# Moving the rounded activations of the down products to other SBUF addresses in a two-layer encoder kernel

## The chip, the cores and the metric

The kernel runs on one NeuronCore of a Trainium2 chip. The metric is the device time of one execution in microseconds (us), median of the runs shown. Addresses in this text are bytes inside one SBUF partition; every tile spans all 128 partitions.

## The reference

256 tokens of width 1024 pass through two layers and a final norm, all in float32. What the change touches are the two feed-forward blocks, and in them the last product.

```python
def swiglu(h, w_gate, w_up, w_down):
    return (jax.nn.silu(h @ w_gate) * (h @ w_up)) @ w_down

def moe_swiglu(h, w_router, b_router, w_gate, w_up, w_down):
    logits = (h @ w_router).astype(jnp.float32) + b_router.astype(jnp.float32)
    top_v, top_i = lax.top_k(logits, TOP_K)            # TOP_K = 2
    top_w = jax.nn.softmax(top_v, axis=-1)
    combine = jnp.sum(jax.nn.one_hot(top_i, N_EXPERTS, dtype=jnp.float32) * top_w[..., None], axis=-2).astype(h.dtype)
    out = jnp.zeros_like(h)
    for e in range(N_EXPERTS):                          # 8 experts
        out = out + combine[..., e:e + 1] * swiglu(h, w_gate[e], w_up[e], w_down[e])
    return out
```

Layer 0 is retention, then the dense `swiglu` with 2816 hidden columns. Layer 1 is attention, then `moe_swiglu` with 3584 hidden columns in each of the 8 experts. Each sub-block is preceded by an RMS norm with a shift and a scale computed from `c`, and its result is gated and added to `x`.

## The kernel before, in words

**Products.** A float32 product is made of three float32r matmuls. The weight tile that came from HBM (`stage`) is rounded by ScalarE to `hi`, and VectorE writes the rest, `lo = stage - hi`. Activations are split the same way, into `..._hi` and `..._lo`. `three` (lines 2006 to 2008) then issues activation-hi x weight-hi, activation-hi x weight-lo and activation-lo x weight-hi into one PSUM bank. In each of them the activation block, 128x128, is the stationary operand, which TensorE loads ahead (the PEld rows), and the 512 columns of `hi` or `lo` are the moving operand. So each matmul of 512 columns is paired with one load of 128x128.

**Units and rings.** Weights arrive in units of 1 MB (128 partitions x 2048 float32). SyncE issues each as two DMAs into one of the 6 slots of `stage` once TensorE has counted that slot free on the semaphore `w_used` (lines 471 to 475); `lo` lies in the same slots, and `hi` has homes of its own (`hi`, and in the expert stage also `hi_m`, `hi_h`, `hi_r`). A unit is 12 matmuls in the expert stage and 24 in the dense layer.

**Dense layer.** The 2816 hidden columns go in 11 chunks of 256, each with two units of gate and up weights and one of down weights. Per chunk (`f_chunk`): gate and up products with `hT_hi`, `hT_lo`, the down products of the chunk before with `faT_hi`, `faT_lo` (24 matmuls, `f_down`), and four transposes of the new hidden values (`f_turn`). ScalarE turns the transposes into `faT_hi` (`f_high_act`, line 954), VectorE into `faT_lo` (`f_low_act`, line 1534). The last chunk uses homes of its own, `faT2_hi` and `faT2_lo`.

**Experts.** Each expert has 7 chunks of 512 hidden columns, 56 in all, and its at most 128 tokens are gathered into `hg_hi`, `hg_lo`. Per chunk: four units of gate and up products (48 matmuls, `e_gate_up`), two units of down products of the chunk before (24 matmuls, `e_down_step`) with `eaT_hi`, `eaT_lo` as stationary operand, and four transposes (`e_turn`, line 2430). ScalarE writes `eaT_hi` (`e_high_act`, line 1135), VectorE writes `eaT_lo` (`e_low_act`, line 1820). The very last chunk uses `eaT2_hi`, `eaT2_lo`.

**Addresses.** Every tile is put at a fixed address by `at(name, shape, offset)`, the offset counted in float32 words from `base`. `R` is the offset of the big work area, and `KW` is 256 words (1024 bytes). A line asserts the place of that area in the pattern of 128 bytes:

```python
base = (nc.sbuf_base + 31) // 32 * 32 + 64
...
assert (base + 4 * R) % 128 == 64
```

With the numbers of this build `base` is 16576, which also leaves 64 when divided by 128. So `stage`, `lo`, `hi`, `hi_m`, `hi_h`, `hi_r`, `hT`, `hg`, `faT` and `eaT` all start 64 bytes into a block of 128 bytes, and so does each of their 512-byte and 2048-byte pieces. Stationary and moving operand of each product therefore start at the same place of that pattern.

Of the kernel before, what the change touches and what calls it, by code (L numbers as in the profile page):

```python
# [10 lines left out]
SEQ = 256  # L11
# [15 lines left out]
F32R = mybir.dt.float32r  # L27
# [29 lines left out]
SLOTS = 128  # L57
# [56 lines left out]
def encoder(nc, x, l0_ada_w, l0_ada_b, l0_norm2_g, l0_ret_w_in, l0_ret_decay_logit,  # L114
# [5 lines left out]
    with ctx:  # L120
# [3 lines left out]
        def at(name, shape, offset, dt=F32):  # L124
            return nc.alloc_sbuf_tensor_at(name, [P] + shape, dt, offset=base + 4 * offset)
# [48 lines left out]
        R = top[0]  # L174
        KW = 256
# [22 lines left out]

        fsil = at("fsil", [TT, FCH], R + 16 * KW)
        fact = at("fact", [TT, FCH], R + 18 * KW)  # L200
        faT_hi = at("faT_hi", [2, SEQ], R + 20 * KW, F32R)
        faT_lo = at("faT_lo", [2, SEQ], R + 22 * KW, F32R)
        faT2_hi = at("faT2_hi", [2, SEQ], R + 24 * KW, F32R)
        faT2_lo = at("faT2_lo", [2, SEQ], R + 26 * KW, F32R)
        hi_q = at("hi_q", [UW], R + 36 * KW, F32R)
# [38 lines left out]
        hi_r = at("hi_r", [UW], R + 24 * KW, F32R)  # L244
        esil = at("esil", [ECH], R + 34 * KW)
        eact = at("eact", [ECH], R + 36 * KW)
        eaT_hi = at("eaT_hi", [4, SLOTS], R + 38 * KW, F32R)
        eaT_lo = at("eaT_lo", [4, SLOTS], R + 40 * KW, F32R)
        dn_hi = at("dn_hi", [D], R + 42 * KW, F32R)
        dn_lo = at("dn_lo", [D], R + 46 * KW, F32R)  # L250
        dnw = [at("dnw0", [CB], R + 34 * KW), at("dnw1", [CB], R + 36 * KW)]
# [2333 lines left out]
```

## Time and profile before

| | us |
|---|---|
| median of 3 runs (1546.7 to 1549.3) | 1547.74 |
| the profiled execution, its device time | 1551.42 |
| span of its instructions | 1549.5 |
| TensorE busy, share of the span | 1496.9, 97% |
| VectorE busy | 1334.4, 86% |
| ScalarE busy | 983.8, 63% |
| moved by DMA | 508.71 MB |

The profile is of one execution, 3.7 us longer than the median; 1.9 us of its time lie outside the span. Stages, read from the timeline: retention to about 258 us, dense layer to about 458 us, attention and router to about 567 us, experts to about 1536 us, then the combination and the final norm. A busy time of TensorE is the union of records that overlap: each matmul of 512 columns has a record of 0.39 us, while they start 0.23 us apart. So the start times tell the pace, and the busy share does not.

### The profile page before, as it was taken

The page shows a single profiled execution, that of the slowest core. Times are in us where ns is not written, and L with a number is a line of the kernel's source. Part 1 is how long each engine was busy: PE and PEld are TensorE (multiplying, and loading weights), DVE is VectorE, ACT ScalarE, POOL GpSimd, SP SyncE. Part 2 cuts the span into 40 slices and gives each one's busy share as a digit, 9 for nine tenths or more (in the row PEclk, how much of TensorE's full clock was granted, in tenths as well). Part 3 has the DMA queues.
Part 4 walks back from the last instruction along what each step waited for, and adds up shares of the span by engine and source line. Part 5 has one row for each costly group of instructions (what it writes and reads, how often), then busy time and mean ns, then how long its engine had stood idle before and what let it go on. Part 6 is the DMA issues. An engine that isn't in the chain of part 4 may idle for free.

```text
span 1549.5 us, 20453 instructions
## 1 busy us (share of the span) xinstructions
PE 1496.9 (97%) x6796; PEld 1220.7 (79%) x6796; DVE 1334.4 (86%) x1072; ACT 983.8 (63%) x814; POOL 212.6 (14%) x188
## 2 busy tenths in 40 slices
PE   7999999999999999999999999999999999999997
PEld 6777677788877787778888888888888887888785
DVE  6899778878889689998988888988988988889898
ACT  4554444443447566677776777777777777777674
POOL 0499700000030011002001002001001000000320
PEclk9999999999999989999999999999999999999999
DMA  9989826898885279999999999999999999999993
GB/s 340 390 303 351 288 87 226 301 307 305 282 275 166 96 283 359 391 346 380 388 368 368 384 370 362 391 370 370 390 367 368 386 367 353 385 381 363 390 392 143
DMA packets 238897, 508.71 MB, mean 328 GB/s; under 512 B 15494, under 2 KB 38150, under 8 KB 238728
## 3 DMA queue, kind: packets, MB, share of 16 engines
q1 hardware_dynamic: 233824, 491.52, 87.2%
q0 software_dynamic: 4448, 14.55, 2.7%
q10 hardware_dynamic: 584, 2.11, 0.3%
q8 instruction: 24, 0.39, 0.1%
q14 instruction: 17, 0.14, 0.0%
HBM read 502.12 MB, written 7.87 MB: 329 GB/s over the span
## 4 chain that ended last, share of the span: by engine, by line
PE 72%; DVE 10%; POOL 7%; DMA 3%; issue 3%; ACT 3%; SPq 1%; DVEq 0%; ACTq 0%; POOLq 0%
PE bank L2006 22%; PE bank L2008 22%; PE bank L2007 22%; DVE lo L1756 3%; PE bank L2430 1%; POOL proj L638 1%; POOL proj L637 1%; DVE lo L1233 1%; POOL ropet L634 1%; POOL ropet L633 1%; POOL ropet L635 1%; POOL proj L636 1%; DMA stage<-in_l_moe_w_up 1%; DMA stage<-in_l_moe_w_gate 1%; PE bank L2112 1%
## 5 line engine op out<-in xcount | busy, mean ns | idle before, releaser
L1756 DVE TENSOR_TENSOR lo<-stage,hi 128x2048 fp32r<-128x2048 f32 x168 | 388.2, 2318 | 44.2 <-ACT hi L1091 43.9
L1091 ACT CAST hi<-stage 128x2048 fp32r<-128x2048 f32 x168 | 321.4, 1914 | 108.3 <-DMA stage<-in_l_moe_w_up 91.8
L2007 PE MATMUL bank<-lo,hg_hi 128*128 128x512 f32 x892 | 347.4, 389 | 0.0
L756 ACT CAST hi<-stage 128x2048 fp32r<-128x2048 f32 x68 | 130.0, 1914 | 108.1 <-PE bank L2008 87.6
L2007 PEld LDWEIGHTS bank<-lo,hg_hi 128*128 128x128 f32 x892 | 167.7, 188 | 33.4
L1233 DVE TENSOR_TENSOR lo<-stage,hi 128x2048 fp32r<-128x2048 f32 x68 | 157.4, 2317 | 24.6 <-ACT hi L756 18.7
L2006 PE MATMUL bank<-hi,hg_hi 128*128 128x512 f32 x448 | 174.5, 389 | 1.4 <-DVE lo L1756 1.4
L2007 PE MATMUL bank<-lo,eaT_hi 128*128 128x512 f32 x448 | 174.4, 389 | 0.0
L2008 PE MATMUL bank<-hi,hg_lo 128*128 128x512 f32 x448 | 174.3, 389 | 0.0
L1756 DVE TENSOR_TENSOR lo<-stage,hi_h 128x2048 fp32r<-128x2048 f32 x56 | 128.3, 2292 | 52.4 <-ACT hi_h L1091 52.2
L2006 PE MATMUL bank<-hi,hT_hi 128*128 128x512 f32 x400 | 162.9, 407 | 2.7 <-DVE hT_lo L1288 2.4
L2007 PE MATMUL bank<-lo,hT_hi 128*128 128x512 f32 x416 | 164.0, 394 | 0.0
L2008 PE MATMUL bank<-hi,hT_lo 128*128 128x512 f32 x400 | 157.6, 394 | 0.0
L1091 ACT CAST hi_r<-stage 128x2048 fp32r<-128x2048 f32 x56 | 107.2, 1913 | 50.4 <-DMA stage<-in_l_moe_w_gate 46.7
L1756 DVE TENSOR_TENSOR lo<-stage,hi_m 128x2048 fp32r<-128x2048 f32 x56 | 128.2, 2290 | 6.3 <-ACT hi_m L1091 5.2
L1756 DVE TENSOR_TENSOR lo<-stage,hi_r 128x2048 fp32r<-128x2048 f32 x56 | 127.9, 2285 | 5.6 <-ACT hi_r L1091 5.3
L1091 ACT CAST hi_m<-stage 128x2048 fp32r<-128x2048 f32 x56 | 107.2, 1915 | 35.1 <-DMA stage<-in_l_moe_w_down 35.0
L1091 ACT CAST hi_h<-stage 128x2048 fp32r<-128x2048 f32 x56 | 107.2, 1913 | 33.6 <-DMA stage<-in_l_moe_w_gate 32.1
L1245 DVE SCALAR_TENSOR_TENSOR ada_acc<-ada_w,cact,ada_acc 128x512 f32<-128x512 f32 x147 | 118.7, 808 | 4.5
L719 POOL DMA_INDIRECT y_rows<-yout,sidx x7 | 10.4, 1484 | 755.3 <-ACT yout L1147 755.3
L2006 PEld LDWEIGHTS bank<-hi,hg_hi 128*128 128x128 f32 x448 | 84.1, 188 | 19.6 <-DVE lo L1756 2.2
L2007 PEld LDWEIGHTS bank<-lo,eaT_hi 128*128 128x128 f32 x448 | 84.2, 188 | 17.6 <-issue 0.5
(367 smaller groups left out, 2793.6 us busy)
## 6 DMA issues: line engine op xcount, KB each, us to landing
stage<-in_l_moe_w_gate SPq DMA_DIRECT2D x224, 512.0 KB, 5.1
stage<-in_l_moe_w_up SPq DMA_DIRECT2D x224, 512.0 KB, 5.7
stage<-in_l_moe_w_down SPq DMA_DIRECT2D x224, 512.0 KB, 5.4
ada_w<-in_l_ada_w SPq DMA_DIRECT2D x40, 1024.0 KB, 5.6
stage<-in_l_ret_w_in SPq DMA_DIRECT2D x48, 512.0 KB, 8.0
stage<-in_l_ffn_w_gate SPq DMA_DIRECT2D x22, 512.0 KB, 7.5
stage<-in_l_ffn_w_up SPq DMA_DIRECT2D x22, 512.0 KB, 8.6
stage<-in_l_ffn_w_down SPq DMA_DIRECT2D x22, 512.0 KB, 8.2
```

What stands on the lines that cost most here:

```text
L633: nc.gpsimd.tensor_tensor(ta, x1, co, ALU.mult)
L634: nc.gpsimd.tensor_tensor(tb, x2, si, ALU.mult)
L635: nc.gpsimd.tensor_tensor(tc, x1, si, ALU.mult)
L636: link(nc.gpsimd.tensor_tensor(x2, x2, co, ALU.mult))
L756: nc.scalar.copy(hi_of(b), stage[:, b % RING, :]).then_inc(hi_done, 1)
L1091: nc.scalar.copy(hi_e(b), stage[:, b % RING, :]).then_inc(hi_done, 1)
L1233: nc.vector.tensor_tensor(lo[:, b % RING, :], stage[:, b % RING, :], hi_of(b).bitcast(F32), ALU.subtract).then_inc(lo_done, 1)
L1245: ins = nc.vector.scalar_tensor_tensor(out=acc, in0=ada_w[:, half, j, :], scalar=cact[:, k:k + 1], in1=acc if k else ada_b[:, :], op0=ALU. ...
L1756: nc.vector.tensor_tensor(lo[:, b % RING, :], stage[:, b % RING, :], hi_e(b).bitcast(F32), ALU.subtract).then_inc(lo_done, 1)
L2006: mm(dst_ap, a_hi, w_hi, start=first, stop=False)
L2007: mm(dst_ap, a_hi, w_lo, start=False, stop=False)
L2008: return mm(dst_ap, a_lo, w_hi, start=False, stop=last)
```

## The change

Four tiles get other addresses; nothing else differs. The instructions of each of the five engines stand in the same order, with the same shapes and the same waits.

```diff
-        faT_hi = at("faT_hi", [2, SEQ], R + 20 * KW, F32R)
-        faT_lo = at("faT_lo", [2, SEQ], R + 22 * KW, F32R)
+        faT_hi = at("faT_hi", [2, SEQ], R + 48 * KW + 16, F32R)
+        faT_lo = at("faT_lo", [2, SEQ], R + 50 * KW + 16, F32R)
...
-        eaT_hi = at("eaT_hi", [4, SLOTS], R + 38 * KW, F32R)
-        eaT_lo = at("eaT_lo", [4, SLOTS], R + 40 * KW, F32R)
+        eaT_hi = at("eaT_hi", [4, SLOTS], R + 58 * KW + 8, F32R)
+        eaT_lo = at("eaT_lo", [4, SLOTS], R + 60 * KW + 8, F32R)
```

| tile | address before | after | place in the 128-byte pattern, before | after |
|---|---|---|---|---|
| `faT_hi` | 184256 | 212992 | 64 | 0 |
| `faT_lo` | 186304 | 215040 | 64 | 0 |
| `eaT_hi` | 202688 | 223200 | 64 | 96 |
| `eaT_lo` | 204736 | 225248 | 64 | 96 |

The moving operands of the same products stay at 64. `faT2` and `eaT2` stay where they were. The tiles whose room is used now (`hi_f` for the dense layer; the router's `wr_hl`, `wr` and `brt`, and a piece of the attention's scratch for the experts) are no longer read when the moved tiles are first written.

## Rows read from the trace of the kernel before

**Rows 1.** The page: busy time, granted clock in 40 slices, chain that ended last.

```profile
PE 1496.9 (97%) x6796; PEld 1220.7 (79%) x6796; DVE 1334.4 (86%) x1072; ACT 983.8 (63%) x814; POOL 212.6 (14%) x188
...
PEclk9999999999999989999999999999999999999999
...
PE 72%; DVE 10%; POOL 7%; DMA 3%; issue 3%; ACT 3%; SPq 1%; DVEq 0%; ACTq 0%; POOLq 0%
```

**Rows 2.** Windows: us, busy of PE, PEld, DVE, ACT, POOL, clock, DMA share, GB/s.

```profile
330.00:440.00 110.00, 110.00 (x487) 89.04 (x486) 88.09 (x81) 44.27 (x37) 5.49 (x7) 1.00 0.89 297
600.00:650.00 50.00, 48.64 (x214) 38.55 (x212) 48.22 (x34) 35.11 (x25) 0.00 (x0) 1.00 1.04 392
1000.00:1100.00 100.00, 99.83 (x459) 82.64 (x458) 87.53 (x51) 74.52 (x51) 4.77 (x6) 1.00 1.02 374
```

**Rows 3.** Waits from 700 to 1500 us: total us, times, longest.

```profile
PE bank L2006 <- DVE lo L1756: 0.9, 1, 0.9
...
SPq L475 <- PE bank L2008: 457.1, 280, 4.2
```

**Rows 4.** Timeline of PE, experts: start us, us, instruction; one chunk's 24 down products.

```profile
1008.00 0.39 PE L2006 MATMUL bank<-hi,eaT_hi 128*128 128x512 f32 x1
1008.23 0.39 PE L2007 MATMUL bank<-lo,eaT_hi 128*128 128x512 f32 x1
1008.46 0.39 PE L2008 MATMUL bank<-hi,eaT_lo 128*128 128x512 f32 x1
...
1013.22 0.39 PE L2008 MATMUL bank<-hi_m,eaT_lo 128*128 128x512 f32 x1
1013.45 0.60 PE L2430 MATMUL bank<-cst,eact 128*128 128x128 f32 x4
```

**Rows 5.** Timeline of PE just behind: the first gate unit after the transposes.

```profile
1013.80 0.48 PE L2006 MATMUL bank<-hi_h,hg_hi 128*128 128x512 f32 x1
1014.12 0.40 PE L2007 MATMUL bank<-lo,hg_hi 128*128 128x512 f32 x1
1014.35 0.40 PE L2008 MATMUL bank<-hi_h,hg_lo 128*128 128x512 f32 x1
1014.59 0.40 PE L2006 MATMUL bank<-hi_h,hg_hi 128*128 128x512 f32 x1
1014.82 0.39 PE L2007 MATMUL bank<-lo,hg_hi 128*128 128x512 f32 x1
1015.04 0.39 PE L2008 MATMUL bank<-hi_h,hg_lo 128*128 128x512 f32 x1
...
1016.43 0.39 PE L2008 MATMUL bank<-hi_h,hg_lo 128*128 128x512 f32 x1
```

**Rows 6.** Timeline of PE, dense layer: first and last of one chunk's 24 down products.

```profile
339.26 0.39 PE L2006 MATMUL bank<-hi,faT_hi 128*128 128x512 f32 x1
...
344.48 0.39 PE L2008 MATMUL bank<-hi,faT_lo 128*128 128x512 f32 x1
```

**Rows 7.** Timeline of PE: float32 records, of 512 columns (dense layer) and of 256.

```profile
327.47 0.59 PE L1984 MATMUL bank<-ada_acc,cst 128*128 128x512 f32 x1
...
344.71 1.02 PE L1984 MATMUL bank<-ada_acc,cst 128*128 128x512 f32 x2
...
494.37 1.89 PE L2278 MATMUL bank<-akT,aqT 128*128 128x256 f32 x8
```

**Rows 8.** Instructions on one tile: count, duration ns min/median/max, first and last start.

```profile
L2007 PE MATMUL bank<-lo,eaT_hi x448: 387/389/397, 592.4 to 1535.6; 128*128 128x512 f32 x150
L2278 PE MATMUL bank<-akT,aqT x32: 377/379/796, 494.4 to 518.3; 128*128 128x256 f32 x32
L1135 ACT CAST eaT_hi<-bank x56: 569/579/594, 581.4 to 1528.1; 128x512 fp32r<-128x512 f32 x56
L1820 DVE TENSOR_TENSOR eaT_lo<-bank,eaT_hi x56: 673/684/693, 587.2 to 1528.8; 128x512 fp32r<-128x512 f32 x56
L1534 DVE TENSOR_TENSOR faT_lo<-bank,faT_hi x11: 683/692/692, 279.5 to 450.1; 128x512 fp32r<-128x512 f32 x11
```

**Rows 9.** Timeline of ACT and DVE: the splits before those down products, and a weight split.

```profile
1000.49 0.58 ACT L1135 CAST eaT_hi<-bank 128x512 fp32r<-128x512 f32 x1
1002.83 0.68 DVE L1820 TENSOR_TENSOR eaT_lo<-bank,eaT_hi 128x512 fp32r<-128x512 f32 x1
1008.44 2.29 DVE L1756 TENSOR_TENSOR lo<-stage,hi_h 128x2048 fp32r<-128x2048 f32 x1 [0.40 <-ACT hi_h L1091]
...
329.30 0.69 DVE L1534 TENSOR_TENSOR faT_lo<-bank,faT_hi 128x512 fp32r<-128x512 f32 x1 [1.76 <-ACT faT_hi L954]
```

## The prediction

> **What bounds the kernel now.** I read the page first: TensorE is busy 97% of the span and holds 72% of the chain that ended last, at nearly the full clock throughout [rows 1]. Busy shares overlap here, so the windows come next: in the dense layer and in the experts' stage TensorE has no idle time, 110.00 of 110 us and 99.83 of 100 us, at a granted clock of 1.00 (2.4 GHz), while VectorE has 12 to 20% left [rows 2]. The waits say who follows whom: from 700 to 1500 us TensorE waits 0.9 us once for `lo`, and SyncE's loads wait 457.1 us for TensorE to free a slot [rows 3]. So the weights' traffic follows TensorE, and the time of these two stages is the number of TensorE's instructions times the distance between their starts. Any change of that distance goes straight into the end.
>
> The distance is read from the timeline. The 24 down products of one expert chunk start at 1008.00 to 1013.22 us, 23 steps in 5.22 us or 0.227 us each [rows 4]; the dense layer's take 339.26 to 344.48, again 0.227 [rows 6]. Two other rows show that 0.227 is no constant of a 512-column matmul. A float32 record takes about twice the time of a float32r one for its columns: two of 512 columns start 1.02 - 0.59 = 0.43 us apart [rows 7]. So one of 256 columns is about the same amount of streaming, beside the same load of 128x128, and those start (1.89 - 0.377) / 7 = 0.216 us apart (0.377 is the shortest single record) [rows 7, 8]. And right behind the transposes the float32r matmuls are uneven: after the first, ten steps from 1014.12 to 1016.43 take 0.231 each, with single ones of 0.24 and of 0.22 [rows 5]. The tiles are the same kinds, the clock is full, and nothing is waited for; afterwards they fall back to 0.227. The record lengths tell it in ns: median 389, shortest 387, longest 397 [rows 8], longer ahead of a long step. I read this as two streams that disturb each other, the moving operand and the stationary operand for the next matmul, both read from SBUF at the same time. In which way depends on how the two are placed to each other. The change moves exactly that: one stream's start in the 128-byte pattern, by 32 bytes for the experts and by 64 in the dense layer.
>
> **The change part by part.** No instruction, wait or DMA is added, removed or moved; the four tiles have other addresses.
>
> 1. *Matmuls concerned.* Experts: 56 chunks, of which the last uses `eaT2`, so 55 x 24 = 1320. Dense layer: 11 chunks, of which the last uses `faT2`, so 10 x 24 = 240. Together 1560, each on the path, so 1 ns on each is 1.56 us. The other matmuls of these stages keep both operands where they were.
>
> 2. *Their new distance.* The trace has no matmul whose operands start at different places of the pattern, so I bound it. Lower end: 0.216, the step with hardly any disturbance [rows 7], 11 ns less, 1560 x 0.011 = -17.2 us. Upper end: each record as the longest of 448, 397 against 389 [rows 8], +8 ns, +12.5 us. Between them lie, in the same kind of instruction, the shortest record (387, -2 ns, -3.1 us) and the unsettled stretch as a whole (0.231, +4 ns, +6.2 us). Sign and size are both unknown. I take -4 ns: the pace today is a repeated pattern that the equal starts allow, both shorter and longer steps exist, and the nearest row below is 387, so the value should lie nearer to it than to 0.216. That gives 1560 x -0.004 = **-6.2 us**.
>
> 3. *Writing the tiles.* ScalarE's split takes 0.58 us and VectorE's 0.68, and 0.69 in the dense layer [rows 8, 9]. `eaT_lo` ends at 1002.83 + 0.68 = 1003.51 and is first used at 1008.00, 4.5 us later [rows 9, 4]; `faT_lo` ends at 329.99 and is used at 339.26 [rows 9, 6]. Twice their duration would still be covered, so this costs 0, whatever the address does to it. Were the cover gone, 0.1 us more in each of the 55 chunks would be 5.5 us.
>
> 4. *What a faster TensorE would meet next.* With 11 ns less a chunk of some 16.8 us loses 24 x 0.011 = 0.26 us, 1.6%. DMA would go from 374 to 380 GB/s, and 392 was moved in another window [rows 2]. VectorE's load goes from 87.5% to 89%. The split that ends at 10.73 (8.44 + 2.29, after 1000) serves the unit that starts at 1013.80 [rows 9, 5], so it is 3 us ahead. The gain would be kept.
>
> 5. *First steps after a change of operand.* A unit of down products follows units whose stationary operand stays at 64. If each such change unsettles the next ten steps by 4 ns, that is 0.04 us x 65 chunks = 2.6 us. At the other end of the down products four transposes unsettle the pace today already, so that end costs 0. I count this in the range, not in the sum.
>
> Sum: the profiled execution took 1551.4 us (span 1549.5 and 1.9 around it), 3.7 above the median. With -6.2 it would take 1545.2, and the median goes from 1547.7 to **1541.5 us**.
>
> **The rivals.** What a measurement of this kernel can tell from no change is 0.2%, 3.1 us, which is 2 ns on each moved matmul.
>
> *A, no change.* The place in the pattern doesn't count, only how much is read: the extra 11 ns belong to every float32r matmul with a load beside it. For it: `hi` and `hi_m` lie 59 KB apart, and the steps run on evenly from one to the other [rows 4]. Against it: the uneven steps of [rows 5] with the same amount read. Or it counts, but by less than 2 ns. Time 1547.7.
> The Trainium skill, "TensorE: Matmul & The Clock Gate", under what each phase is for, speaks for this rival: TensorE has two independent read ports, and loading the next tile's weights takes no SBUF bandwidth from the running matmul. By that rule no address could matter. The trace agrees only in part, since 0.216 and 0.227 both have such a load beside them.
>
> *B, slower.* The even 0.227 exists because both streams start at the same place; with 32 or 64 bytes between them the down products never settle and run like the stretch behind the transposes, 0.231 [rows 5]: +4 ns, +6.2 us, 1553.9; with the longest record throughout 1560.2. It decides from 2 ns up. For it: 0.227 is below the mean of the unsettled steps, so today's placement is rather a good one, and two of the three other places could well be worse. Against it: single steps of 0.22 show that better relations exist, and the unsettled steps end by themselves after some ten.
>
> *C, one of each.* The experts' 32 bytes and the dense layer's 64 go different ways. 1320 against 240 matmuls: the experts decide the sign, and the dense layer's part is at most 240 x 0.011 = 2.6 us. This makes no case of its own.
>
> *D, much faster.* The disturbance goes away wholly, 0.216: 1530.5 us. It is the far end of the forecast's case.
>
> **How the numbers follow.** Faster, my forecast with D as its end: 0.43. The step can plainly change, and 11 ns are there to be had against 4 to 8 to be lost. No change: 0.25. Slower: 0.32. The predicted time is the likeliest case's, 1541.5. The range must take in the better part of both signs: down to 1531, just short of D, and up to 1556, which holds B at 0.231 together with term 5 (1556.5 at most), but not the longest record throughout. The forecast's own range is 1531 to 1545. These chances and ends rest on bounds, not on a row that shows such a product.
>
> **What would show it.** In the timeline of the changed kernel the 24 down products of a chunk should span 23 x 0.223 = 5.13 us in place of 5.22, in the experts and in the dense layer, with records a few ns off 389; the gate and up products must stay at 0.227, and the window from 1000 to 1100 should hold some more matmuls than 459. Right with A: 5.22 again. Right with B: steps of 0.22 to 0.24 in turn, some 5.3 us. I am wrong if the down products' pace is unchanged and the time isn't, or if a wait of TensorE for `eaT_lo` or `lo` turns up.

## The result and the profile after

The changed kernel takes 1558.25 us (median of 5 runs, 1555.95 to 1559.89) against 1547.74 of the kernel before (median of 5 runs by now, 1546.70 to 1551.17). The ratio is 1.0057, with a 95% interval of 1.0040 to 1.0074: slower by 0.6%. The ratio answers to 8.8 us; the two medians of five lie 10.5 us apart. The prediction said 1541.5 and faster, with an upper end of 1556. It is wrong in sign, and the time lies 2 us outside its range.

| | before | after |
|---|---|---|
| median, us | 1547.74 | 1558.25 |
| the profiled execution, us | 1551.42 | 1559.49 |
| span, us | 1549.5 | 1557.7 |
| TensorE busy, us | 1496.9 | 1508.1 |
| VectorE / ScalarE busy, us | 1334.4 / 983.8 | 1334.4 / 985.2 |

The page of the changed kernel, the lines that answer to [rows 1]:

```profile
span 1557.7 us, 20453 instructions
...
PE 1508.1 (97%) x6796; PEld 1225.8 (79%) x6796; DVE 1334.4 (86%) x1072; ACT 985.2 (63%) x814; POOL 205.4 (13%) x188
...
PEclk9999999999999979999999999999999999999999
...
PE 72%; DVE 11%; POOL 7%; DMA 4%; ACT 3%; issue 3%; SPq 1%; ACTq 0%; DVEq 0%; POOLq 0%
```

The counts of instructions are the same. VectorE's busy time is too, and ScalarE's is 1.4 us longer. TensorE's grew by 11.2 us. The windows after (columns as in [rows 2]):

```profile
330.00:440.00 110.00, 110.00 (x484) 88.38 (x483) 87.24 (x81) 44.56 (x37) 4.18 (x5) 1.00 0.89 294
560.00:600.00 40.00, 39.19 (x174) 33.86 (x175) 32.41 (x51) 21.30 (x16) 6.84 (x8) 0.84 0.70 255
600.00:1520.00 920.00, 914.34 (x4122) 748.60 (x4121) 809.00 (x466) 675.54 (x448) 56.14 (x48) 1.00 1.01 374
1000.00:1100.00 100.00, 100.00 (x457) 82.36 (x456) 86.27 (x50) 73.48 (x51) 4.82 (x6) 1.00 1.00 370
```

And two windows of the kernel before that were not shown above:

```profile
560.00:600.00 40.00, 38.67 (x182) 32.97 (x182) 33.44 (x50) 21.48 (x16) 6.09 (x6) 0.91 0.77 276
600.00:1520.00 920.00, 911.65 (x4143) 750.29 (x4142) 814.88 (x470) 679.66 (x453) 63.20 (x48) 1.00 1.01 375
```

At a granted clock of 1.00 (2.4 GHz) throughout, the 920 us of the experts' stage hold 21 matmuls fewer, although TensorE has 2.7 us less idle time in them. The place is seen in the timeline of TensorE, one expert chunk of the changed kernel (columns as in [rows 4]):

```profile
1011.47 0.40 PE L2008 MATMUL bank<-hi,hg_lo 128*128 128x512 f32 x1
1011.71 0.39 PE L2006 MATMUL bank<-hi,eaT_hi 128*128 128x512 f32 x1
1011.94 0.39 PE L2007 MATMUL bank<-lo,eaT_hi 128*128 128x512 f32 x1
1012.17 0.40 PE L2008 MATMUL bank<-hi,eaT_lo 128*128 128x512 f32 x1
1012.40 0.40 PE L2006 MATMUL bank<-hi,eaT_hi 128*128 128x512 f32 x1
...
1017.07 0.39 PE L2008 MATMUL bank<-hi_m,eaT_lo 128*128 128x512 f32 x1
1017.30 0.60 PE L2430 MATMUL bank<-cst,eact 128*128 128x128 f32 x4
```

From 1011.71 to 1017.07 the 23 steps take 5.36 us, 0.233 each, where [rows 4] gave 0.227. In the unrounded starts they repeat 232 and 235 ns, and over the 54 undivided groups of 24 down products the median pace is 233.1 ns against 226.7 before. The dense layer's go the same way, 5.37 / 23 = 0.233 against 0.227 in [rows 6]:

```profile
339.46 0.40 PE L2006 MATMUL bank<-hi,faT_hi 128*128 128x512 f32 x1
...
344.83 0.39 PE L2008 MATMUL bank<-hi,faT_lo 128*128 128x512 f32 x1
```

The gate and up products, whose operands did not move, keep 0.227. The tiles are written as fast as before; instructions on one tile, after (columns as in [rows 8], and the same but for the matmul's median, 395 for 389 ns):

```profile
L2007 PE MATMUL bank<-lo,eaT_hi x448: 389/395/397, 595.8 to 1544.0; 128*128 128x512 f32 x150
L1135 ACT CAST eaT_hi<-bank x56: 572/582/602, 584.8 to 1536.4; 128x512 fp32r<-128x512 f32 x56
L1820 DVE TENSOR_TENSOR eaT_lo<-bank,eaT_hi x56: 676/684/692, 590.6 to 1537.0; 128x512 fp32r<-128x512 f32 x56
L1534 DVE TENSOR_TENSOR faT_lo<-bank,faT_hi x11: 683/692/693, 279.4 to 451.1; 128x512 fp32r<-128x512 f32 x11
```

So 1320 down products of the experts at 6.5 ns more are 8.6 us, and 240 of the dense layer 1.6. Of the experts' 8.6 only a part arrives. The waits of TensorE from 560 to 1545 us, before (total us, times, longest):

```profile
PE bank L2430 <- DVE eact L1811: 3.3, 5, 0.8
PE bank L2006 <- issue: 3.1, 4, 2.0
PE bank L2465 <- DVE dn_lo L1852: 1.6, 2, 0.9
PE bank L2006 <- DVE lo L1756: 1.4, 2, 0.9
```

and after:

```profile
PE bank L2430 <- DVE eact L1811: 2.5, 5, 0.8
PE bank L2006 <- issue: 2.3, 1, 2.3
PE bank L2006 <- DVE lo L1756: 0.9, 1, 0.9
```

("issue" stands for idle time for which the profile shows no releaser.) With three smaller ones (0.7, 0.5 and 0.5 before; 0.6 and 0.5 after) they sum to 11.1 us before and 6.8 after. In this pair a slower TensorE meets more of the others' results ready, and 8.6 - 4.3 = 4.3 us are left; the window says 21 x 0.222 = 4.7 (920 us / 4143 a matmul).

One pair of profiles is weak ground for that, because the waits differ from execution to execution too: they sum to 8.2 and 8.9 us in e1 and e8 below, where the pace is that of the kernel before, and to 8.3, 7.2 and 7.3 in e2 to e4, where it is the slower one. More profiles settle how much arrives. From its first to its last start, the experts' down product with `lo` (the line of [rows 8]) takes 939.9 to 943.8 us, mean 941.8, in the six profiles with an even 0.227 there (before, e1, e6, e8, e15, e17), and 945.0 to 948.2, mean 946.3, in the eight at 0.233 (after, e2 to e5, e7, e11, e13). So of some 8.5 us about 4.5 arrive. The listed waits are 9.8 us on average in the first group and 7.8 in the second, which is about 2 of the 4 us that don't arrive; where the others go isn't shown.

In the dense layer 1.2 of the 1.6 us arrive: from the first to the last down product it is 171.2 us before and 172.4 after.

A third piece isn't in the moved products. From the last attention product to the first expert product, before:

```profile
545.50 0.40 PE L2008 MATMUL bank<-hi,oT_lo 128*128 128x512 f32 x1
...
566.84 0.73 PE L2481 MATMUL bank<-hi,hg_hi 128*128 128x512 f32 x1
```

and after:

```profile
546.28 0.39 PE L2008 MATMUL bank<-hi,oT_lo 128*128 128x512 f32 x1
...
570.26 0.73 PE L2481 MATMUL bank<-hi,hg_hi 128*128 128x512 f32 x1
```

That is 21.3 us against 24.0, with the granted clock from 560 to 600 us at 0.84 instead of 0.91 of 2.4 GHz, so more of this stretch ran at 1.2 GHz. In all: 4.7 + 1.2 + 2.6 = 8.5 us, against 8.2 between the two spans.

The longer interlude goes with a slowed dense layer. In the seven profiles whose dense down products are at 0.227 (before, e1, e2, e8, e10, e13, e14) it is always short, 21.3 to 21.7 us. Of the thirteen in which they are slower, nine have it long, 23.3 to 24.2 us (after, e5 to e7, e11, e12, e15 to e17), and four short, 21.4 to 21.8 (e3, e4, e9, e18). The granted clocks of all the runs, profiled or not, point the same way. Their mean is 0.9856 over the changed kernel's five runs and 0.9878 over the 31 of the kernel before that stand beside e1; of the versions with several runs, the four with an even dense layer have means of 0.9873 to 0.9885 and the ten with a slower one 0.9858 to 0.9872. So the 2.6 us most likely belong to the change and not to the one execution. By what path a dense layer that is 1 us later makes this stretch longer is not shown.

### The profile page after: what moved, and what is told of

The parts are those of the page before. It is cut to its first block, busy times and chain, and to the rows that moved or that the text cites. A ratio compares the mean times of both kernels' runs of the same rounds, so it can differ in the third digit from the quotient of the medians.

```text
span 1557.7 us, 20453 instructions
## 1 busy us (share of the span) xinstructions
PE 1508.1 (97%) x6796; PEld 1225.8 (79%) x6796; DVE 1334.4 (86%) x1072; ACT 985.2 (63%) x814; POOL 205.4 (13%) x188
## 4 chain that ended last, share of the span: by engine, by line
PE 72%; DVE 11%; POOL 7%; DMA 4%; ACT 3%; issue 3%; SPq 1%; ACTq 0%; DVEq 0%; POOLq 0%
PE bank L2006 22%; PE bank L2008 22%; PE bank L2007 22%; DVE lo L1756 3%; DMA stage<-in_l_moe_w_up 2%; PE bank L2430 1%; POOL proj L638 1%; POOL proj L637 1%; POOL ropet L634 1%; POOL ropet L633 1%; POOL ropet L635 1%; POOL proj L636 1%; DVE lo L1233 1%; PE bank L2112 1%; DVE ada_acc L1605 1%
```

## Experiments

The theory, after the result: a down product is slowed when its stationary tile starts at another place of the pattern than its moving tile. The first rivals: the far region of SBUF does it, or one stage does it all. In each diff only the lines that replace those of the kernel before are shown; its own lines are the removed ones of the change above. "Difference" is by how many bytes the stationary tile starts behind its moving operand's place. "Step" is the distance between two starts, here in us; a unit or chunk is measured from its first to its last down product, 23 steps. Ratios are to the kernel before on the same chip, with 95% intervals.

### e1: the new homes, the old place in the pattern

```diff
+faT_hi = at("faT_hi", [2, SEQ], R + 48 * KW + 0, F32R)
+faT_lo = at("faT_lo", [2, SEQ], R + 50 * KW + 0, F32R)
+eaT_hi = at("eaT_hi", [4, SLOTS], R + 58 * KW + 0, F32R)
+eaT_lo = at("eaT_lo", [4, SLOTS], R + 60 * KW + 0, F32R)
```

> The four tiles go to the new region of the change (58 and 60 KB, 48 and 50 KB into the work area), but start at place 64 of the 128-byte pattern as before. Theory (the place of the stationary operand relative to the moving one sets the distance of the matmuls): all down products 0.227 us apart again, 1547.7 us. Rival (the region of SBUF, or what lies there, counts, not the place in the pattern): 0.233 as in the changed kernel, about 1558 us. Second rival (writing the tiles there is slower and delays TensorE): waits of TensorE for eaT_lo, time above 1550.

1548.75 us, ratio 0.9999 [0.9978, 1.0019]. Timeline of TensorE, the same unit as above:

```profile
1005.36 0.39 PE L2006 MATMUL bank<-hi,eaT_hi 128*128 128x512 f32 x1
...
1010.58 0.39 PE L2008 MATMUL bank<-hi_m,eaT_lo 128*128 128x512 f32 x1
```

5.22 us, 0.227 a step. The dense layer is at 0.227 too. With the same region and difference 0 the whole loss is gone, so the region is excluded and the place is what counts.

### e2: only the experts' tiles, 32 bytes on

```diff
+eaT_hi = at("eaT_hi", [4, SLOTS], R + 58 * KW + 8, F32R)
+eaT_lo = at("eaT_lo", [4, SLOTS], R + 60 * KW + 8, F32R)
```

> Only the experts' tiles move, to place 96 (32 bytes on); the dense layer's stay at home. Theory (6.6 ns more on each moved matmul, on the path): experts 1320 x 6.6 ns = +8.7 us, 1556.4 us, dense layer back to 0.227. Rival (part of the loss lies in how the streams settle elsewhere, or the two parts overlap with other waits): a sum that does not add up, below +6 or the whole +10.5 us.

1554.01 us, 1.0032 [1.0015, 1.0049], that is 5.0 us. Experts 0.233, dense layer 0.227; windows and, in the timeline, the dense unit:

```profile
600.00:1520.00 920.00, 914.77 (x4131) 748.81 (x4130) 812.44 (x466) 677.23 (x450) 55.74 (x48) 1.00 1.01 374
```

```profile
338.99 0.39 PE L2006 MATMUL bank<-hi,faT_hi 128*128 128x512 f32 x1
...
344.20 0.39 PE L2008 MATMUL bank<-hi,faT_lo 128*128 128x512 f32 x1
```

The two stages are independent, each follows its own tiles. The experts' 8.6 us of longer steps arrive as 5.0, less than the 8.7 that I expected.

### e3: the two differences exchanged, 64 for the experts, 32 for the dense layer

```diff
+faT_hi = at("faT_hi", [2, SEQ], R + 48 * KW + 8, F32R)
+faT_lo = at("faT_lo", [2, SEQ], R + 50 * KW + 8, F32R)
+eaT_hi = at("eaT_hi", [4, SLOTS], R + 58 * KW + 16, F32R)
+eaT_lo = at("eaT_lo", [4, SLOTS], R + 60 * KW + 16, F32R)
```

> The two shifts are swapped: experts' tiles 64 bytes on (place 0), dense layer's 32 bytes on (place 96). Theory (only equality with the moving operand counts, any other place costs the same): experts and dense layer both near 0.233 and about 1558 us. Rival (each place has its own price, and the stages differ): the experts' distance takes the dense layer's value of the changed kernel, and a value clearly off 0.233 in one of the two shows which place is better.

1556.32 us, 1.0045 [1.0030, 1.0060]. Experts (1014.98 - 1009.61) / 23 = 0.2335, dense layer 0.233. Both differences cost the same in both stages.

### e4: both 96 bytes on

```diff
+faT_hi = at("faT_hi", [2, SEQ], R + 48 * KW + 24, F32R)
+faT_lo = at("faT_lo", [2, SEQ], R + 50 * KW + 24, F32R)
+eaT_hi = at("eaT_hi", [4, SLOTS], R + 58 * KW + 24, F32R)
+eaT_lo = at("eaT_lo", [4, SLOTS], R + 60 * KW + 24, F32R)
```

> Experts' and dense layer's tiles 96 bytes on (place 32, that is 32 bytes before the moving operand's place). Theory (only equality counts): 0.233, about 1558 us. Rival (the order counts: whoever starts behind the other in the pattern avoids it): a distance below 0.227 on this side, down to 0.216, 1531 us, since the other side, 32 on, gave 0.233.

1556.4 us, 1.0042 [1.0018, 1.0065], 0.234 in both stages. So all three other multiples of 32 within 128 bytes are bad.

### e5: 4 bytes for the experts, 8 for the dense layer

The tiles are slices of slightly larger ones. Here, and in e6, e11 and e12, the `lo` tile stands 128 bytes further than `hi`, which I took for the same place; e13 shows that it isn't. The pairs (4, 132) and (8, 136) are meant in this run.

```diff
+faT_hi = at("faT_hi", [2 * SEQ + 32], R + 48 * KW + 0, F32R)[:, 2:2 + 2 * SEQ].rearrange("p (k n) -> p k n", k=2)
+faT_lo = at("faT_lo", [2 * SEQ + 32], R + 50 * KW + 32, F32R)[:, 2:2 + 2 * SEQ].rearrange("p (k n) -> p k n", k=2)
+eaT_hi = at("eaT_hi", [4 * SLOTS + 32], R + 58 * KW + 0, F32R)[:, 1:1 + 4 * SLOTS].rearrange("p (k n) -> p k n", k=4)
+eaT_lo = at("eaT_lo", [4 * SLOTS + 32], R + 60 * KW + 32, F32R)[:, 1:1 + 4 * SLOTS].rearrange("p (k n) -> p k n", k=4)
```

> Fine shifts: the experts' tiles start 4 bytes behind the moving operand's place (68 in the pattern), the dense layer's 8 bytes behind (72). Theory (only the full equality of the places gives the even 0.227): both near 0.233, about 1558 us. Rival (a block of some bytes counts as one place, so a few bytes are no difference): 0.227 for one or both, 1548 us. Second rival (a small lag is better than none): below 0.227 and below 1547.

1556.29 us, 1.0044 [1.0030, 1.0057]; 0.233 and 0.231. Read with the caution above; e18 repeats it with both tiles alike.

### e6: 16 bytes for the experts, 48 for the dense layer (`lo` at 144 and 176)

```diff
+faT_hi = at("faT_hi", [2 * SEQ + 32], R + 48 * KW + 0, F32R)[:, 12:12 + 2 * SEQ].rearrange("p (k n) -> p k n", k=2)
+faT_lo = at("faT_lo", [2 * SEQ + 32], R + 50 * KW + 32, F32R)[:, 12:12 + 2 * SEQ].rearrange("p (k n) -> p k n", k=2)
+eaT_hi = at("eaT_hi", [4 * SLOTS + 32], R + 58 * KW + 0, F32R)[:, 4:4 + 4 * SLOTS].rearrange("p (k n) -> p k n", k=4)
+eaT_lo = at("eaT_lo", [4 * SLOTS + 32], R + 60 * KW + 32, F32R)[:, 4:4 + 4 * SLOTS].rearrange("p (k n) -> p k n", k=4)
```

> The experts' tiles start 16 bytes behind the moving operand's place, the dense layer's 48 bytes behind. Theory (any unequal place costs 6 to 7 ns per matmul): 0.233 in both, about 1558 us. Rival (places in between those tried behave otherwise): any other value, below 0.227 would be a gain of up to 14 us for the experts.

1552.76 us, 1.001 [0.999, 1.003]. Experts 0.227 and even, dense layer 0.230. The expected 0.233 missed in both. Place 16 is as good as equality or nearly so, and so is the `lo` tile's 144 beside it; no pace is shorter.

### e7: one of the two tiles moved, `eaT_lo` by 32 bytes, in the dense layer `faT_hi` by 32

```diff
+faT_hi = at("faT_hi", [2, SEQ], R + 48 * KW + 8, F32R)
+faT_lo = at("faT_lo", [2, SEQ], R + 52 * KW, F32R)
+eaT_hi = at("eaT_hi", [4, SLOTS], R + 58 * KW + 0, F32R)
+eaT_lo = at("eaT_lo", [4, SLOTS], R + 60 * KW + 8, F32R)
```

> Experts: eaT_hi stays at place 64, eaT_lo goes to 96; dense layer the other way round, faT_hi at 96 and faT_lo at 64. Two of three products use the hi part as stationary operand. Theory (each load that starts unequal to the moving operand that streams beside it costs its own few ns): experts about one third of the loss, mean 0.229; dense layer two thirds, 0.231. Rival (one unequal operand breaks the even pace for all three): 0.233 in both.

1556.68 us, 1.0052 [1.0037, 1.0067]. The experts' products in the timeline:

```profile
1011.74 0.39 PE L2006 MATMUL bank<-hi,eaT_hi 128*128 128x512 f32 x1
1011.97 0.40 PE L2007 MATMUL bank<-lo,eaT_hi 128*128 128x512 f32 x1
1012.21 0.39 PE L2008 MATMUL bank<-hi,eaT_lo 128*128 128x512 f32 x1
1012.43 0.40 PE L2006 MATMUL bank<-hi,eaT_hi 128*128 128x512 f32 x1
1012.67 0.40 PE L2007 MATMUL bank<-lo,eaT_hi 128*128 128x512 f32 x1
```

The unrounded steps repeat 233, 239 and 228 ns, behind the product in line 2006, 2007 and 2008; that is 0.233 on average, where only one load in three has an unequal place. That load, of `eaT_lo`, starts together with the product of line 2007 (both at 1012.67), so the longest step is the one beside which it runs. But the step of 233 ns has an equal load beside it and is 6 ns over 227 all the same. So the unequal load lengthens its own step by 12 ns and upsets another.

The dense layer, where two loads of three are unequal, is at 0.2315, less than with one in the experts. The theory's 0.229 and 0.231 holds for the dense layer alone, the rival's 0.233 for the experts alone. The price does not grow with the number of unequal loads, and by e6, where one load in three stands at 144 and nothing is lost, it isn't paid for every kind of unequal place.

### e8: every tile 64 bytes lower, at place 0 of the pattern

```diff
-base = (nc.sbuf_base + 31) // 32 * 32 + 64
+base = (nc.sbuf_base + 31) // 32 * 32
-assert (base + 4 * R) % 128 == 64
+assert (base + 4 * R) % 128 == 0
```

> The whole memory plan moves down by 64 bytes: every tile, stationary and moving, starts at place 0 in place of 64. Theory (only the relation between the two operands counts): 0.227 everywhere and 1547.7 us within 0.2 per cent. Rival (the absolute place counts, 64 is a good one): another distance for all 5000 and more float32r matmuls, 0.233 would be about +36 us.

1549.23 us, 1.0003 [0.9989, 1.0016], 0.2265 and 0.227. The absolute place doesn't matter between these two, 64 bytes apart, only how the two operands stand to each other.

### e9: the moving side 32 bytes away, the work area left

```diff
-base = (nc.sbuf_base + 31) // 32 * 32 + 64
+base = (nc.sbuf_base + 31) // 32 * 32 + 32
-R = top[0]
+R = top[0] + 8
```

> The other operand is shifted: everything below the work area, so stage, lo, hi, hi_m and hi_h, starts at place 32, while hT, hg, faT, eaT and hi_r keep 64. The down products then have their stationary operand 32 bytes behind the moving one, as in the changed kernel, and so have nearly all float32r products of the kernel. Theory (only the relation counts): down products at 0.233 as in the changed kernel, gate and up products at 0.233 too, some 5400 matmuls with 6.6 ns more each, about +35 us, 1583 us. Rival (it is the stationary operand's own place that costs): 0.227 and 1548 us, since no activation moved.

1570.16 us, 1.0143 [1.0125, 1.0162]. The float32r products that pair `hi` and `lo` with a tile of the work area are now slowed, the gate and up products among them. (`hi_r` lies in the work area and keeps difference 0; in its unit, where only the `lo` products are unequal, the step is 0.231.) Groups of instructions by line (busy us, mean ns of one, idle before), e9:

```profile
L2007 PE MATMUL bank<-lo,hg_hi 128*128 128x512 f32 x892 | 352.8, 396 | 0.0
...
L2007 PE MATMUL bank<-lo,eaT_hi 128*128 128x512 f32 x448 | 177.1, 395 | 0.0
```

and in e8:

```profile
L2007 PE MATMUL bank<-lo,hg_hi 128*128 128x512 f32 x892 | 347.5, 390 | 0.0
...
L2007 PE MATMUL bank<-lo,eaT_hi 128*128 128x512 f32 x448 | 174.3, 389 | 0.0
```

The effect comes whichever of the two sides is moved; the difference is 32 both times. The size is smaller than I expected, 21 us and not 34. The window of the experts' stage in e9:

```profile
600.00:1520.00 920.00, 918.26 (x4092) 742.51 (x4091) 802.37 (x457) 668.30 (x445) 54.54 (x48) 1.00 1.00 370
```

Idle time fell from 920 - 911.65 = 8.4 us to 1.7, and about 10 of the 72 products of a chunk were unsettled before as well and had nothing to lose. 4143 x 0.006 x 62/72 - 6.7 = 14.7 us; the window shows 51 x 0.222 = 11.3. Part of this difference is the scatter of single profiles: from its first to its last start the experts' down product with `lo` takes 955.5 us here, against 943.2 in the kernel before, but 940.3 in e1 and 939.9 in e8, which run at the same pace, so the loss is 12.3 to 15.6 us. Why no more than this arrives is open, as above.

### e10 and e14: fewer columns to load, 64 and 96

The experts' down products are computed for 64 (e10) or 96 (e14) of the 128 token slots only. e10:

```diff
+ins = three(bank[0:64, 4 + c2, :], hi_a[:, 2 * g + k, 0:64], lo_a[:, 2 * g + k, 0:64], h[:, k, cols],
+ins = three(bank[0:64, 4 + c2, :], eaT2_hi[:, k, 0:64], eaT2_lo[:, k, 0:64], h[:, k % 2, cols], l[:, k % 2, cols],
```

> The experts' down products use only 64 of the 128 columns of the stationary operand (half of the tokens' results is left out); places are equal, the moving operand is whole. Theory (what the distance has above 0.2133 or 0.216 is the price of reading the stationary operand beside the moving one): the excess halves, 0.220 us apart in the experts' down products, some 9 us less in all. Rival (the excess is a fixed price of changing the stationary operand): 0.227 as before, same time.

1553.22 us in one run (before: 1548.87). Instructions on one tile, e10:

```profile
L2007 PEld LDWEIGHTS bank<-lo,eaT_hi x448: 133/134/138, 592.7 to 1537.5; 128*64 128x64 f32 x150
...
L2007 PE MATMUL bank<-lo,eaT_hi x448: 387/392/399, 592.9 to 1537.8; 128*64 128x512 f32 x150
```

The load takes 134 ns and not 188, and yet the step is (1014.95 - 1009.66) / 23 = 0.230, uneven. Both theories fail here: with half as much to load I expected 0.220, the rival 0.227. e14 has `0:96` and `bank[0:96]` in the same two places:

> The experts' down products load 96 of the 128 columns of the stationary operand (a quarter of the tokens' results is left out), places equal. Theory (only the full load beside equal starts locks into the even pace, as the half load at 0.230 suggests): uneven, 0.228 to 0.234, no gain. Rival (the price goes by the bytes loaded, and the half load was an odd case): 0.2235, some 4 us less.

1552.68 us in one run (before: 1549.54), again 0.230. So less load does not mean less disturbance, and an equal start alone is not enough for the even rhythm. That it is the load that counts is not separated here: both runs also write fewer partitions of the bank, 64 and 96 of 128.

### e11: 112 for the experts, 80 for the dense layer (`lo` at 240 and 208)

```diff
+faT_hi = at("faT_hi", [2 * SEQ + 32], R + 48 * KW + 0, F32R)[:, 20:20 + 2 * SEQ].rearrange("p (k n) -> p k n", k=2)
+faT_lo = at("faT_lo", [2 * SEQ + 32], R + 50 * KW + 32, F32R)[:, 20:20 + 2 * SEQ].rearrange("p (k n) -> p k n", k=2)
+eaT_hi = at("eaT_hi", [4 * SLOTS + 32], R + 58 * KW + 0, F32R)[:, 28:28 + 4 * SLOTS].rearrange("p (k n) -> p k n", k=4)
+eaT_lo = at("eaT_lo", [4 * SLOTS + 32], R + 60 * KW + 32, F32R)[:, 28:28 + 4 * SLOTS].rearrange("p (k n) -> p k n", k=4)
```

> Experts' tiles start 112 bytes behind the moving operand's place (16 before the next one), the dense layer's 80. Theory (16 behind gave 0.227, every other place tried 0.230 to 0.234, none below): 0.230 to 0.235 in both, experts part +4 to +10 us. Rival (a relation exists that is better than equality): below 0.2265.

1556.7 us, 1.0040 [1.0026, 1.0054]; 0.233 in both.

### e12: 12 for the experts, 120 for the dense layer (`lo` at 140 and 248)

```diff
+faT_hi = at("faT_hi", [2 * SEQ + 32], R + 48 * KW + 0, F32R)[:, 30:30 + 2 * SEQ].rearrange("p (k n) -> p k n", k=2)
+faT_lo = at("faT_lo", [2 * SEQ + 32], R + 50 * KW + 32, F32R)[:, 30:30 + 2 * SEQ].rearrange("p (k n) -> p k n", k=2)
+eaT_hi = at("eaT_hi", [4 * SLOTS + 32], R + 58 * KW + 0, F32R)[:, 3:3 + 4 * SLOTS].rearrange("p (k n) -> p k n", k=4)
+eaT_lo = at("eaT_lo", [4 * SLOTS + 32], R + 60 * KW + 32, F32R)[:, 3:3 + 4 * SLOTS].rearrange("p (k n) -> p k n", k=4)
```

> Experts' tiles 12 bytes behind the moving operand's place, the dense layer's 120 (8 before). Theory (starts off a multiple of 16 bytes never reach the even pace, 4 behind gave 0.233 and 8 gave 0.231): 0.229 to 0.234 in both. Rival (a relation exists that is better than equality): below 0.2265.

1553.48 us, 1.0033 [1.0023, 1.0043]; 0.229 and 0.2335.

### e13: 128 and 256 bytes, is the pattern 128 long?

```diff
+faT_hi = at("faT_hi", [2, SEQ], R + 48 * KW + 64, F32R)
+faT_lo = at("faT_lo", [2, SEQ], R + 50 * KW + 64, F32R)
+eaT_hi = at("eaT_hi", [4, SLOTS], R + 58 * KW + 32, F32R)
+eaT_lo = at("eaT_lo", [4, SLOTS], R + 60 * KW + 32, F32R)
```

> Experts' tiles start 128 bytes behind the place of before (counted beyond one block of 128), the dense layer's 256. Theory (the pattern has a period of 128 bytes, so both are equality again): 0.227 in both, 1548 us. Rival (the pattern is longer, 256 bytes or more): the experts' down products at 0.230 to 0.235, 1553 to 1558 us, the dense layer at 0.227.

1552.13 us, 1.0020 [1.0009, 1.0031]. The experts' unit, 128 bytes on, takes 5.36 us; the dense layer's, 256 on, 5.21:

```profile
1008.76 0.40 PE L2006 MATMUL bank<-hi,eaT_hi 128*128 128x512 f32 x1
...
1014.12 0.39 PE L2008 MATMUL bank<-hi_m,eaT_lo 128*128 128x512 f32 x1
```

```profile
336.08 0.39 PE L2006 MATMUL bank<-hi,faT_hi 128*128 128x512 f32 x1
...
341.29 0.39 PE L2008 MATMUL bank<-hi,faT_lo 128*128 128x512 f32 x1
```

128 bytes on costs as much as 32; 256 costs nothing. So the pattern is 256 bytes long, not the 128 that the kernel's assertion names, and the theory's 0.227 missed for the experts. In the kernel before all these tiles are equal in 256 too (16576, 184256 and 202688 all leave 192), which is why its products are at 0.227.

### e15: 240 for the experts, 224 for the dense layer

```diff
+faT_hi = at("faT_hi", [2 * SEQ + 32], R + 48 * KW + 56, F32R)[:, 0:0 + 2 * SEQ].rearrange("p (k n) -> p k n", k=2)
+faT_lo = at("faT_lo", [2 * SEQ + 32], R + 51 * KW + 56, F32R)[:, 0:0 + 2 * SEQ].rearrange("p (k n) -> p k n", k=2)
+eaT_hi = at("eaT_hi", [4 * SLOTS + 32], R + 57 * KW + 56, F32R)[:, 4:4 + 4 * SLOTS].rearrange("p (k n) -> p k n", k=4)
+eaT_lo = at("eaT_lo", [4 * SLOTS + 32], R + 60 * KW + 56, F32R)[:, 4:4 + 4 * SLOTS].rearrange("p (k n) -> p k n", k=4)
```

> Experts' tiles 240 bytes on (16 before equality, if the pattern is 256 bytes), the dense layer's 224 (32 before). Theory (only equality and a lag of up to 16 bytes of the stationary operand give the even pace): 0.230 to 0.235 in both. Rival (the pattern is symmetric about equality): the experts at 0.227, as 16 behind. Second rival (a lead is better than equality): below 0.2265.

1553.75 us, 1.0034 [1.0020, 1.0049]. At 240, 16 before equality, the experts are even again (1008.96 to 1014.17, 0.2265); at 224 the dense layer is at 0.2335. The time is nevertheless longer than e13's: this profile has the longer interlude, and the granted clock of all five runs is 0.985 or 0.986, against a mean of 0.9885 over e13's ten.

### e16: 192 for the experts, 160 for the dense layer

```diff
+faT_hi = at("faT_hi", [2 * SEQ + 32], R + 48 * KW + 40, F32R)[:, 0:0 + 2 * SEQ].rearrange("p (k n) -> p k n", k=2)
+faT_lo = at("faT_lo", [2 * SEQ + 32], R + 51 * KW + 40, F32R)[:, 0:0 + 2 * SEQ].rearrange("p (k n) -> p k n", k=2)
+eaT_hi = at("eaT_hi", [4 * SLOTS + 32], R + 57 * KW + 48, F32R)[:, 0:0 + 4 * SLOTS].rearrange("p (k n) -> p k n", k=4)
+eaT_lo = at("eaT_lo", [4 * SLOTS + 32], R + 60 * KW + 48, F32R)[:, 0:0 + 4 * SLOTS].rearrange("p (k n) -> p k n", k=4)
```

> Experts' tiles 192 bytes on, the dense layer's 160. Theory (no place beats equality): 0.230 to 0.235 in both, about 1556 us. Rival (a better place exists on this side): below 0.2265 and below 1547 us.

1552.83 us, 1.0029 [1.0013, 1.0044]; 0.2287 and 0.2335. With both tiles alike, 192 is the cheapest of the far places, and still no better than equality.

### e17: 16 and 128 bytes, both tiles alike

```diff
+faT_hi = at("faT_hi", [2 * SEQ + 8], R + 48 * KW + 32, F32R)[:, 0:0 + 2 * SEQ].rearrange("p (k n) -> p k n", k=2)
+faT_lo = at("faT_lo", [2 * SEQ + 8], R + 51 * KW + 32, F32R)[:, 0:0 + 2 * SEQ].rearrange("p (k n) -> p k n", k=2)
+eaT_hi = at("eaT_hi", [4 * SLOTS + 8], R + 58 * KW + 0, F32R)[:, 4:4 + 4 * SLOTS].rearrange("p (k n) -> p k n", k=4)
+eaT_lo = at("eaT_lo", [4 * SLOTS + 8], R + 61 * KW + 0, F32R)[:, 4:4 + 4 * SLOTS].rearrange("p (k n) -> p k n", k=4)
```

> Experts: both tiles 16 bytes on; dense layer: both tiles 128 bytes on. Theory (within 16 bytes of equality the pace is even, as at 240; at 128 it is not, and the pattern is 256 bytes long): experts 0.227, dense layer 0.230 to 0.235. Rival (the even pace at 16 needed the lo tile 128 bytes further): experts uneven.

One run, 1553.93 (before, one run too: 1552.77). Experts (1017.24 - 1012.03) / 23 = 0.2265, even; dense layer 0.2326. Both as expected.

### e18: 4 and 8 bytes, both tiles alike

```diff
+faT_hi = at("faT_hi", [2 * SEQ + 8], R + 48 * KW + 0, F32R)[:, 2:2 + 2 * SEQ].rearrange("p (k n) -> p k n", k=2)
+faT_lo = at("faT_lo", [2 * SEQ + 8], R + 51 * KW + 0, F32R)[:, 2:2 + 2 * SEQ].rearrange("p (k n) -> p k n", k=2)
+eaT_hi = at("eaT_hi", [4 * SLOTS + 8], R + 58 * KW + 0, F32R)[:, 1:1 + 4 * SLOTS].rearrange("p (k n) -> p k n", k=4)
+eaT_lo = at("eaT_lo", [4 * SLOTS + 8], R + 61 * KW + 0, F32R)[:, 1:1 + 4 * SLOTS].rearrange("p (k n) -> p k n", k=4)
```

> Experts: both tiles 4 bytes on; dense layer: both tiles 8 bytes on. Theory (within 16 bytes of equality the pace is even): 0.227 in both, and the unevenness of the earlier kernel with 4 and 8 came from its lo tiles. Rival (it is not the distance but being a multiple of 16 bytes that keeps the pace): uneven, 0.229 to 0.235, in both.

One run, 1550.71 (before: 1552.77); this single time tells nothing, the pace does:

```profile
1007.94 0.40 PE L2006 MATMUL bank<-hi,eaT_hi 128*128 128x512 f32 x1
...
1013.28 0.40 PE L2008 MATMUL bank<-hi_m,eaT_lo 128*128 128x512 f32 x1
```

5.34 / 23 = 0.232 at 4 bytes, 0.231 at 8. Four bytes away is nearly as dear as 32, while sixteen are free. The expected 0.227 missed in both: nearness to equality is not what counts.

### All places together

| difference, bytes | step, ns (first to last start / 23) | from |
|---|---|---|
| 0, 256 | 227 | before, e1, e8, e13 |
| 16, 240 | 227 | e17, e15 |
| 4, 8 | 232, 231 | e18 |
| 32 | 233 | after, e2, e3, and e9 from the other side |
| 64, 96 | 233 to 234 | after, e3, e4 |
| 128 | 233 | e13, e17 |
| 160, 224 | 233 to 234 | e16, e15 |
| 192 | 229 | e16 |
| 0, but 64 or 96 columns loaded | 230 | e10, e14 |
| `hi` and `lo` apart: 16 and 144 | 227 | e6 |
| 12 and 140; 48 and 176 | 229; 230 | e12; e6 |
| 4 and 132; 8 and 136 | 233; 231 | e5 |
| 80 and 208; 112 and 240; 120 and 248 | 232; 233; 233 | e11; e11; e12 |
| 0 and 32; 32 and 0 | 233; 231.5 | e7 |

No place that was tried is better than equality, and no version is faster than the kernel before.

## Why the prediction was wrong

**What bounds the kernel** was right: TensorE's steps, at full clock, with the others following. But "any change of that distance goes straight into the end" was too strong, and it rests on a reading that left out a row. The view of the waits from 700 to 1500 us has two of TensorE, and [rows 3] shows the second alone:

```profile
PE bank L2006 <- issue: 3.1, 4, 2.0
PE bank L2006 <- DVE lo L1756: 0.9, 1, 0.9
```

So it waited 4.0 us there and not 0.9, and 11.1 us from 560 to 1545. About half of the experts' 8.6 us did not arrive. For a slowdown the small waits count: they are room that it can use up, here about 2 us on average.

**Term 1**, the 1560 matmuls, was right: only they changed pace, the rest stayed at 0.227 (e2 shows the stages apart). But "each on the path" was not, as above.

**Term 2 failed, and it decides the case**: "I take -4 ns". It is +6.5. That the pace depends on how stationary and moving operand are placed to each other was right (e1, e9); reading a record's length as the step was too, 395 for 389 ns beside 233 for 227. The step that failed is how its sign was chosen. I let the value be drawn by the nearest row below, the shortest record of 387 ns, since "both shorter and longer steps exist". But single steps of 0.22 between steps of 0.24 are parts of a rhythm and not a pace. In the unrounded starts the ten steps of [rows 5] are 235, 233, 236, 224, 231, 236, 228, 233, 230 and 227 ns: a single one lies below the even pace, by 3 ns, and the average is 0.231. That average was the only row in which products of this form ran unevenly at all, and it pointed to +4. Likewise 0.216 came from float32 products of another form, and no place reached it. The runs put every other place between 0.227 and 0.234.

**Term 3**, writing the tiles: right, 582 and 684 ns against 579 and 684.

**Term 4**, "the gain would be kept": there was none, so it wasn't tested.

**Term 5**, unsettled first steps after a change of operand: not seen. Averaged over the chunks from 600 to 1520 us, the changed kernel's down products start with steps of 231 and 229 ns and then repeat 235 and 232 to the end. The gate products behind the transposes settle no later than before: before, the uneven steps are nine in 28 of 52 chunks and five in 20; after, they are five or six in 43 of 53.

**Rival A** fell: e1 against the changed kernel is the test, the same region and amount read, 9.5 us apart (1558.25 and 1548.75). The rule that I weighed there from the Trainium skill, "TensorE: Matmul & The Clock Gate", under "Step-by-step: what each phase is for", says that loading the next tile takes no SBUF bandwidth from the running matmul. Taken as I took it, that no address can matter, it isn't borne out here: the relation of the two addresses costs 6.5 ns of 227. e10, where a load of 134 ns instead of 188 changed the step, doesn't fit it either, as far as it is the load that counts there.

**Rival B** was the case, with the behaviour as written: the products never settle, and steps of 232 and 235 ns come in turn. Its price of +4 ns was too small, the steps of 0.233 are worse than the stretch behind the transposes, and its 1553.9 is 4.3 us below the measured time. That it comes so near is partly luck: its sum lets every matmul's price arrive, of which about half did in the experts' stage, and it has no term for the 2.6 us of the longer interlude at half clock. Its condition, "both streams start at the same place", held, but in a pattern of 256 bytes. I took 128 from the kernel's assertion, without a row that bore it out.

**Rival C**: 32 and 64 bytes go the same way. **Rival D**: no run comes near 0.216.

**The chances** were 0.43 to 0.32 for the wrong side, on bounds of -11 and +8 ns. The lower bound was four times as far as anything the same kind of product showed (2 ns in the shortest record, 3 ns in the shortest step of [rows 5]), and it pulled the chance with it. The upper end of 1556 was also drawn half a us below the 1556.5 that it was said to hold.

**Left open:** why 256 bytes, why 16 either side is free, why 4 and 8 are not, why 192 costs 2 ns where its neighbours cost 6 or 7, why `lo` at 144 does no harm in e6, and why e10 and e14 are uneven at equal starts. No run shows what in the chip makes the pattern. How the slower dense layer makes the interlude before the experts longer is open too.

## What to carry to other kernels

When float32r matmuls with a load beside each follow one another at full clock, list for each kind of product where its stationary and its moving tile start, modulo 256 bytes, and keep the two equal; move both or neither. When bounding an unknown pace, go by the mean over a stretch of the same instruction, not by its shortest single step, and don't let a row of another data type be the end. Before saying that a change per instruction goes straight into the end, add up every wait of the stage, since a slowdown can use them up, and take more than one profile of each kernel before putting a number on that.

## What the runs showed of the hardware

- The step of a float32r matmul of 512 columns with a load of 128 columns beside it depends on the relation of the two start addresses: 227 ns at difference 0, 231 to 234 ns at 4, 8, 32, 64, 96, 128, 160 and 224 bytes, 229 at 192, with a period of 256 bytes (e13). A difference of exactly 16 bytes either way costs nothing (e15, e17), while 4 and 8 bytes give 232 and 231 ns (e18).
- Moving all tiles by 64 bytes (e8, 0.2265) or the stationary ones by 20 and 28 KB (e1, 0.227) changes nothing, and either operand may be the one that is shifted (e9, 0.233).
- One load in three that is 32 bytes off gives steps of 228, 233 and 239 ns, the longest beside the unequal load (e7, experts); two in three give 231.5 on average (e7, dense layer), and one in three at 144 bytes, the others at 16, gives an even 227 (e6).
- A load of 64 columns takes 134 ns instead of 188, but with it, and with results for 64 columns only, the step becomes longer, 0.230 (e10).
- Of some 8.5 us that TensorE's steps lost in the experts' stage, about 4.5 arrived (mean 941.8 against 946.3 us over six and eight profiles); its listed waits shrank by about 2 (9.8 against 7.8).
- With a slower dense layer the stretch before the experts took 23.3 to 24.2 us instead of 21.3 to 21.7 in nine profiles of thirteen, more of it at 1.2 GHz (granted clock 0.84 against 0.91 from 560 to 600 us).
